# By-head norm, gate and turn of the second layer's attention output, with its gate kept on chip

## The reference, cut to what matters

```python
    a = p[:, 0] - lam * p[:, 1]                 # two softmaxes per head
    o = einsum('bhqk,bkhd->bqhd', a, v)
    o = rmsnorm(o, subln) * (1.0 - lambda_init) # per token and head, over 128 columns
    y = o.reshape(B, S, DIFF_WIDTH) * silu(gate)
    return y @ w_out
# and around it
    h = h + rmsnorm(y, norm_post[i])
```

## Time and profile before

| | us |
|---|---|
| runs of before | 2479.74, 2485.02, 2482.21 |
| median | 2482.21 |
| profiled execution, whole | 2479.8 |
| its span on the core | 2478.0 |
| PE busy | 2193.9 (89%) |
| DVE, ACT, POOL busy | 953.9, 873.6, 865.2 |

### The profile page before, as it was taken

How to read it: one execution, slowest core, us unless ns; L and a number is a source line. 1 busy time by engine, 2 the same in 40 slices (tenths; PEclk the granted TensorE clock), 3 DMA queues, 4 the chain that set the end, 5 groups by cost and what they waited for, 6 DMA issues and landing times. The chain is left out here.

```text
span 2478.0 us, 26013 instructions
## 1 busy us (share of the span) xinstructions
PE 2193.9 (89%) x10048; PEld 1736.3 (70%) x10048; DVE 953.9 (38%) x1603; ACT 873.6 (35%) x1740; POOL 865.2 (35%) x454
## 2 busy tenths in 40 slices
PE   4998999999957997857999999887987998999998
PEld 3877788888846775646677777675765456887876
DVE  1333334633453356553253411247552642210121
ACT  2544445655353554323232122231322222321231
POOL 3422233333314322244344433342224313444442
PEclk9999999999978999978999999898998998999999
DMA  4312122222332211222352233232223432332321
GB/s 154 100 53 69 52 84 71 86 86 81 129 110 75 90 52 58 70 85 85 102 149 89 86 86 94 73 102 69 81 79 124 131 113 66 96 103 85 102 90 64
DMA packets 130634, 221.32 MB, mean 89 GB/s; under 512 B 8744, under 2 KB 58456, under 8 KB 130304
## 3 DMA queue, kind: packets, MB, share of 16 engines
q1 hardware_dynamic: 110720, 168.63, 22.5%
q0 software_dynamic: 9104, 32.66, 4.0%
q10 hardware_dynamic: 10688, 18.35, 2.1%
HBM read 199.40 MB, written 19.62 MB: 88 GB/s over the span
## 5 line engine op out<-in xcount | busy, mean ns | idle before, releaser
L2238 POOL TENSOR_TENSOR lo_ring<-raw_ring,hi_ring 128x1024 fp32r<-128x1024 f32 (+1 forms) x304 | 732.0, 2430 | 1188.3 <-ACT hi_ring L1891 1188.2
L855 PE MATMUL bank<-xh,hi_ring 128*128 128x512 f32 x1472 | 601.7, 409 | 5.4 <-DVE xl L1337 3.3
L855 PE MATMUL bank<-xh,lo_ring 128*128 128x512 f32 x1472 | 582.4, 396 | 0.0
L855 PE MATMUL bank<-xl,hi_ring 128*128 128x512 f32 x1472 | 581.6, 395 | 0.0
L1891 ACT CAST hi_ring<-raw_ring 128x1024 fp32r<-128x1024 f32 (+1 forms) x304 | 303.4, 1046 | 512.9 <-PE bank L855 491.2
L855 PEld LDWEIGHTS bank<-xh,hi_ring 128*128 128x128 f32 x1472 | 282.5, 192 | 77.2 <-issue 18.5
L855 PEld LDWEIGHTS bank<-xh,lo_ring 128*128 128x128 f32 x1472 | 281.0, 191 | 61.5
L855 PEld LDWEIGHTS bank<-xl,hi_ring 128*128 128x128 f32 x1472 | 282.5, 192 | 57.8 <-issue 2.6
L855 PE MATMUL bank<-hi_ring,xh 128*128 128x512 f32 (+1 forms) x608 | 249.8, 411 | 11.4 <-POOL lo_ring L2238 6.4
L855 PE MATMUL bank<-hi_ring,xl 128*128 128x512 f32 (+1 forms) x608 | 242.2, 398 | 0.0
L855 PE MATMUL bank<-lo_ring,xh 128*128 128x512 f32 (+1 forms) x608 | 242.2, 398 | 0.0
(11 more groups left out here) (246 smaller groups left out, 2477.7 us busy)
## 6 DMA issues: line engine op xcount, KB each, us to landing
raw_ring<-in_ffn_w_in SPq DMA_DIRECT2D x176, 256.0 KB, 3.1
raw_ring<-in_dil_w_in SPq DMA_DIRECT2D x80, 512.0 KB, 3.7
raw_ring<-in_ffn_w_out SPq DMA_DIRECT2D x44, 512.0 KB, 3.8
raw_ring<-in_diff_w_in SPq DMA_DIRECT2D x32, 512.0 KB, 3.7
raw_ring<-in_w_in SPq DMA_DIRECT2D x32, 512.0 KB, 3.7
arena<-scratch_heads POOLq DMA_DIRECT2D x4, 1584.0 KB, 13.9
scratch_gates<-arena ACTq DMA_DIRECT2D x24, 256.0 KB, 2.1
arena<-scratch_gates POOLq DMA_DIRECT2D x24, 256.0 KB, 3.8
```

The costliest lines, as they stand in the source:

```text
L855: ins = T.matmul(bank[pb][:, 0:S if p.form == "feature" else p.cols], lhsT, rhs, start=(k == 0 and m == 0), stop=(k == p.K - 1 and m == le ...
L2238: G.tensor_tensor(lo, raw_ring[:, p % RAW, 0:q.kq * q.n], hi.bitcast(F32), ALU.subtract).then_inc(lowered, 1)
```

## The change

The list of jobs is different in four places, and four pieces of work are made anew.

- In the attention, the scores of tile n are put before the combine of tile n-1, the values of tile n-2 get the next step for themselves, and the turn of tile n-1 comes a step later, at the head of the step that holds the scores of tile n+1. This holds for both halves of the layer.
- Once a head's output is written, ACT squares it in four pieces of 128 columns with a sum each (o_square). DVE and POOL make the factor at the next head (o_mean).
- The gate goes to mix_gate, which lies in the first half's query and key tiles, and stays there. The store, the fetch and scratch_silu are gone. A head's output is multiplied by factor and gate at once on DVE, four instructions of 128 columns (o_weigh): for heads 0 to 3 behind macs 10, 12, 14 and 16 of the gate panels, for heads 4 to 7 after them.
- A head is turned into one bank by four transposes (o_turn), rounded with subln as the scale on ACT, and lowered on DVE with subln as the scale (o_lower). subln is now one value for each partition. Heads 0 to 3 are turned at once after the attention. Then come the four macs of the first step of the first y panel, which need chunks 0 to 3 only. Then follow, for each of the heads 4 to 7, o_weigh, o_turn and o_lower, and the second step waits for all of them (the field late).
- Both barriers go, the one after the attention and the one ahead of the output projection. The row norm_post now lies where o_sq was, and is loaded after the last squares.

```diff
-def finish_layer(plan, w, row_name, next_name):
-    plan.job("over", False)
-    plan.job("row", row_name)
-    for c in range(2):
+def finish_layer(plan, w, row_name, next_name, first=0):
+    if first == 0:
+        plan.job("over", False)
+        plan.job("row", row_name)
+    for c in range(first, 2):
...
         for n in range(N + 2):
+            if n < N:
+                plan.job("f_score", u, *jobs[n], banks=(4, 5))
             if 1 <= n <= N:
                 plan.job("f_combine", u, *jobs[n - 1])
-            if n < N:
-                plan.job("f_score", u, *jobs[n], banks=(4, 5))
+            yield
+            if n >= 2:
+                hh, i = jobs[n - 2]
+                plan.job("f_values", u, hh, i, banks=(7,) if i == 0 else ())
+                if i == NT - 1:
+                    plan.job("o_square", 4 * u + hh)
+                if i == 0 and hh:
+                    plan.job("o_mean", 4 * u + hh - 1)
             yield
             if 1 <= n <= N:
                 plan.job("f_turn", u, *jobs[n - 1], banks=(6,))
-            if n >= 2:
-                hh, i = jobs[n - 2]
-                plan.job("f_values", u, hh, i, banks=(7,) if i == 0 else ())
-            yield
+        plan.job("o_mean", 4 * u + 3)
...
-    interleave(gate_panels(plan, w, 3 * D, 1), side, 2.2)
-    plan.job("over", True)
-    plan.job("o_gate")
-    for n in range(NT):
-        plan.job("o_scale", n)
-    for n in range(NT + 1):
-        if n < NT:
-            plan.tile_parts("o_tile", n)
-        if n:
-            plan.job("lower", n - 1)
+    owed = 0.0
+    for step, _ in enumerate(gate_panels(plan, w, 3 * D, 1)):
+        owed += 2.2
+        while owed >= 1.0:
+            owed -= 1.0
+            next(side, None)
+        if step >= 9 and step % 2:
+            plan.job("o_weigh", (step - 9) // 2)
+    run_all(side)
+    plan.job("row", "post1")
+
+    def turn_head(h):
+        return ((f"drained{4 + h % 4}", plan.job("o_turn", h, banks=(4 + h % 4,))[0]),)
+
+    ready = [turn_head(h) for h in range(4)]
+    for h in range(4):
+        plan.job("o_lower", h)
+    plan.parts = (sum(ready, ()),) * NT
+    late = [(), (), (), ()]
+    main = plan.panel("y", "diff_w_out", 0, 512, "tile", at=(0,), late=late)
+    for _ in range(4):
+        next(main)
+    ready = []
+    for h in range(4, 8):
+        plan.job("o_weigh", h)
+        ready.append(turn_head(h))
+        plan.job("o_lower", h)
+    late[:] = [sum(ready, ())] * NT
+    run_all(main)
+    plan.parts = ((), (), (), ())
...
+                elif kind == "o_turn":
+                    h = a[0]
+                    T.wait_ge(o_weighed, h + 1)
+                    empty(4 + h % 4, job.use[0])
+                    for n in range(NT):
+                        ins = T.transpose(tile(bank[4 + h % 4], n), tile(O[:, n, :], h), ident)
+                    ins.then_inc(filled[4 + h % 4], 1)
...
+            def o_weigh(h):
+                V.wait_ge(o_rstd_made, h + 1)
+                V.wait_ge(drained[3], gate_panel[1, h // 4].use[3])
+                for n in range(NT):
+                    o_ = tile(O[:, n, :], h)
+                    ins = V.scalar_tensor_tensor(o_, o_, o_rms[:, 4 * h + n:4 * h + n + 1], tile(tile_gate(n, h // 4), h % 4), ALU.mult, ALU.mult)
+                ins.then_inc(o_weighed, 1)
+
+            def o_lower(job, h):
+                b = 4 + h % 4
+                V.wait_ge(o_rounded, h + 1)
+                V.scalar_tensor_tensor(xl[:, h, :], bank[b][:, :], subln, xh[:, h, :].bitcast(F32), ALU.mult, ALU.subtract).then_inc(drained[b], 1)
...
+                elif kind == "o_square":
+                    h = a[0]
+                    A.wait_ge(drained[7], use_of["f_values", 4 * NT * (h // 4) + NT * (h % 4)][0])
+                    if h:
+                        A.wait_ge(o_squared, h)
+                    for n in range(NT):
+                        ins = A.activation(tile(o_sq, n), tile(O[:, n, :], h), ACT.Square, accum_out=o_rms[:, 4 * h + n:4 * h + n + 1])
+                    ins.then_inc(o_squared, 1)
```

More of the change, by code:

```diff
@@ L83 @@
 Job = namedtuple("Job", "kind at n use")
-Panel = namedtuple("Panel", "kind at n w cols K form src use needs base")
+Panel = namedtuple("Panel", "kind at n w cols K form src use needs base late")
 Step = namedtuple("Step", "panel pieces k0 last end ahead")
@@ L119, in piece, with panel @@
         return len(self.pieces) - 1
-    def panel(self, kind, w, c0, cols, form, at=(), K=KC, src="x", k_first=0, halves=1, after=(), base=0):
+    def panel(self, kind, w, c0, cols, form, at=(), K=KC, src="x", k_first=0, halves=1, after=(), base=0, late=((),) * 4):
         parted = src in ("x", "hidden")
@@ L131, in panel @@
             needs = self.parts
-        self.panels.append(Panel(kind, at, n, w, cols, K, form, src, use, needs, base))
+        self.panels.append(Panel(kind, at, n, w, cols, K, form, src, use, needs, base, late))
         for first in range(0, K, 2 * KP):
@@ L554, in make_plan @@
     differential_layer(plan)
-    finish_layer(plan, "diff_w_out", "post1", "mix")
+    finish_layer(plan, "diff_w_out", "post1", "mix", first=1)
     ready = feed_forward(plan, "ffn1_w_in", "ffn1_w_out", before_hybrid(plan))
@@ L829, in mac @@
                     for name_value in p.needs[b]:
+                        T.wait_ge(*ready_value(name_value))
+                else:
+                    for name_value in p.late[b]:
                         T.wait_ge(*ready_value(name_value))
@@ L1260, in consume @@
                 m = 4 * p.n + o
-                if p.kind == "gate" and p.at[0] == 0:
+                if p.kind == "gate":
                     g = tile_gate(o, p.at[1])
@@ L1798, in vector_program @@
                     f_values(job, *a)
[L1799 to L1804, removed]
-                elif kind == "o_tile":
-                    o_tile(job, a[0])
+                elif kind == "o_mean":
+                    o_mean(a[0])
+                elif kind == "o_weigh":
+                    o_weigh(a[0])
+                elif kind == "o_lower":
+                    o_lower(job, a[0])
                 elif kind == "lot" and a[0] == 1:
@@ L1895, in consume @@
                 m = 4 * p.n + o
-                if p.kind == "gate" and p.at[0] == 0:
+                if p.kind == "gate":
                     A.wait_ge(filled[o], p.use[o])
                     A.activation(tile_gate(o, p.at[1]), psum, ACT.Tanh, scale=0.5).then_inc(gate_tanhed, 1)
-                elif p.kind == "gate":
-                    b, k = o % 2, 4 * p.at[1] + o
-                    A.wait_ge(filled[o], p.use[o])
-                    if k < 2:
-                        A.wait_ge(roped, 64)
-                    else:
-                        A.wait_ge(silu_stored[b], 16 * (k // 2))
-                    A.activation(rope_a[:, b, :], psum, ACT.Tanh, scale=0.5).then_inc(gate_tanhed, 1)
                 elif p.kind == "v":
@@ L2113, in scalar_program @@
                     ins.then_inc(third_weighed, 1)
-                elif kind in ("norm_tile", "mix", "o_tile"):
+                elif kind in ("norm_tile", "mix"):
                     round_tile(job, a[0])
@@ L2133, in scalar_program @@
                     copy_out(6, job.use[0], f_pt[:, job.n % 2, 0:nk], bank[6][:, 0:nk])
-                elif kind == "o_scale":
-                    A.activation(o_sq[:, a[0], :], O[:, a[0], :], ACT.Square).then_inc(o_squared, 1)
+                elif kind == "o_square":
[6 more added lines that the diff above has]
+                    ins.then_inc(o_squared, 1)
+                elif kind == "o_turn":
+                    h = a[0]
+                    A.wait_ge(filled[4 + h % 4], job.use[0])
+                    A.activation(xh[:, h, :], bank[4 + h % 4][:, :], ACT.Copy, scale=subln).then_inc(o_rounded, 1)
                 elif kind == "lot" and a[0] == 1:
@@ L2278, in gpsimd_program @@
                         splits(s)
-                    p = panels[steps[s].panel]
-                    if steps[s].last and p.kind == "gate" and p.at[0] == 1:
-                        layer, c = p.at
-                        G.wait_ge(drained[o], p.use[o])
-                        G.dma_start(scratch_silu[layer, o * P:(o + 1) * P, c * 512:(c + 1) * 512],
-                                    rope_a[:, o % 2, :]).then_inc(silu_stored[o % 2], 16)
                 elif kind == "over":
@@ L2305, in gpsimd_program @@
                 elif kind == "lambda":
-                    G.dma_start(rowv, I["rows"][0, ROWS["subln"][0]:ROWS["lk2"][1]].partition_broadcast(P)).then_inc(row_landed, 16)
-                elif kind == "o_gate":
-                    for b in range(2):
-                        G.wait_ge(silu_stored[b], 16 * 4)
-                    G.dma_start(o_gate, scratch_silu[1].rearrange("(n p) c -> p n c", p=P)).then_inc(o_gate_landed, 16)
-                elif kind == "o_scale":
-                    n = a[0]
-                    rstd(small[:, 16 + 8 * n:24 + 8 * n], o_meaned, n + 1, o_rstd_made)
```

(8 more changed lines are left out.)

48 lines of the change are left out of this document (20 added, 28 removed).

## The result

The changed kernel took 2470.62 us, the median of four runs (2469.68 to 2470.86). The kernel before took 2480.97, the median of its four runs. The ratio is 0.9948, with a 95% interval of 0.9932 to 0.9965, so the change gains 9 to 17 us of 2481. I had forecast 2461 (2450 to 2475). The time lies in the range, but the gain is 10 us where I had 21. The profiled execution took 2470.61, with a span of 2468.7 against 2478.0.

A forecast was written before the change was run, and what follows sets the result against it. PE and its pauses bound the kernel. Gains of 12.6 after the attention, 9 beside the gate panels and 0 beside the projections, 21.6 off 2479.8, with 2.4 added for the median, gave 2461 us (2450 to 2475).

The forecast's parts named there:

- the waits only move: Rival, attention beside the gate panels: PE's waits shift from f_turn to f_values, behind ACT, gaining 0; 2470 us, chance 0.20.
- part 2: Attention beside the gate panels: the later turn cuts PE's waits from 20.2 to about 13 us; gain 9, bounds 0 to 20.
- Part 1: After the attention, last values to end of output projection: 63.8 us against 76.4, gain 12.6, bounds 7.5 to 13.6.
- first step with its slow start: Output projection's first 48 matmuls: 10.9 us at full clock, plus 0.8 for half a low-clock restart.
- chain: Between the projection's first and second steps: heads 4 to 7 go one after another, three links of 3.3 us; 12.3 us.
- rest of y with its slow start: Output projection's second step and second panel: 144 matmuls, 32.7 us, plus 1.6 for the low-clock restart.
- The note that the early step hides nothing: After the attention: the early first step hides only head 4's weighing; with all turns ahead the sum would be 62.8 us.
- the rival of a longer chain: Rival, after the attention: links of 5 us take 5 us from the gain; 2466 us, chance 0.10.
- The 2 us for the clock: Beside the gate panels: low clock after waits costs 3 us of slower work before the change, 1 after.
- The eight stores bring nothing: Beside the gate panels: the gate's eight stores ended no wait of PE, so removing them brings nothing.
- Part 3: Attention beside the projections: waits for the combine mostly go, waits for the copy come; gain 0, bounds -5 to +5.
- POOL holds DVE: Rival, gate panels' stretch: POOL's subtractions hold up weighings and combines on DVE, about 7 us more; 2468 us, chance 0.07.

The follow-up runs named there:

- chain_first: The changed kernel with heads 4 to 7 weighed, turned and lowered ahead of the output projection's first four macs; 2468.21 us, ratio 0.994.
- old_order: The changed kernel with the attention's order of before in both halves, the rest of the change kept; 2472.01 us, ratio 0.9957.
- old_first_half: The changed kernel with the attention's order of before only in the half beside the projections; 2468.86 us, ratio 0.9931.
- turns_between: The changed kernel with weighings of heads 4 to 7 ahead of the first output step, their turns between its macs; 2457.06 us, ratio 0.9894.
- before_again: The kernel before, unchanged, run once more for a second trace; 2475.24 us, measured once.
- order_alone: The kernel before with only the new order of the attention in both halves; 2479.91 us, ratio 0.9976.
- after_again: The changed kernel, unchanged, run again for a second trace; 2471.28 us, ratio 0.9949.
- values_later: The changed kernel with the attention's values one tile later, tile n-3 where tile n-2 stood; 2468.12 us, ratio 0.9937.
- turns_between_again: The same kernel as turns_between, unchanged, run once more beside both_best; 2455.96 us, ratio 0.9873.
- both_best: The changed kernel with the edits of turns_between and old_first_half together; 2452.02 us, ratio 0.9867.

## Why the prediction was right or wrong

**What bounds the kernel.** Right: PE and its pauses; what was found lies in a pause or in the clock.

**The number.** The time lies in the range, but only half of the gain came. It stands almost on the 2470 of the rival "the waits only move", and that is chance: part 2 did not give 0. The two parts of the stage fell short by some 3 us each, and 6 us were lost outside it.

**Part 1, 12.6 forecast, 9.5 measured.** The mechanism was right to the link, the size was off in all four terms:

| term | forecast | measured |
|---|---|---|
| last values to first matmul of y | 5.5 | 5.7 |
| first step with its slow start | 0.8 + 10.9 | 12.6 |
| chain | 12.3 | 13.1 |
| rest of y with its slow start | 1.6 + 32.7 | 35.5 |
| sum | 63.8 | 66.9 |

The chain had three links, 3.2, 3.3 and 3.7 us, where I had 3.3; the last two turns took 1.12 at the half clock. The clock was the larger miss. I halved the first restart because its pause is short (3.87 us); eight matmuls at about 0.43 us and a few between cost it 1.7 all the same. The restart behind the chain cost 2.8, twelve matmuls at 0.43, where the earlier trace rows show eight. The note that the early step hides nothing is confirmed (chain_first: 64.5, where I had 62.8). What I failed to do was to ask of the chain, which I had named as the main point, whether it had to be: the rival of a longer chain weighed links of 5 us, and none of my cases took the chain for mere order.

**Part 2, 9 forecast, 7.8 measured.** The waits of the stretch are 11.4 us (6.5 and 4.9) where I had some 13 (5 and 8), a good size. The 2 us for the clock did not come: 0.95 before, 0.94 after, and PE was busy 0.8 us longer. "The eight stores bring nothing" is confirmed by old_order.

**Part 3, 0 forecast, a loss of 2.1 measured.** Inside the bounds. The copy behind ACT's work cost 6.4 us in four waits, where I had 5.4; the waits for the combine that I let go kept 3.8 of their some 6. With the old order there the whole attention is equally long, by fewer waits and a slower PE (old_first_half), so parts 2 and 3 are better read as one: 9 forecast, 5.7 measured. Of the difference 2 is the clock and 1.3 are waits: 7.2 less were forecast (20.2 to 13), 5.9 less measured.

**POOL holds DVE.** The longest combine took 2.63 us before, at the end of PE's wait of 6.43, and 1.93 after. One of 512 columns, 0.75 alone, took 1.80 after and ended a wait of PE of 2.13. In the tail it shows plainly: the first two of head 4's weighing instructions took 2.72 beside a subtraction of POOL's, where all four take 1.13 without POOL.

```profile
1064.84 2.72 DVE L1512 SCALAR_TENSOR_TENSOR arena<-arena,small 128x128 f32<-128x128 f32 x2
1064.91 2.50 POOL L2277 TENSOR_TENSOR lo_ring<-raw_ring,hi_ring 128x1024 fp32r<-128x1024 f32 x1 [1.49 <-ACT hi_ring L1926]
```

By the Trainium skill, "SBUF — State Buffer", section "Who interferes with whom", such a pair holds each other off; this row agrees for DVE, whose two end just after POOL's one. The four are done at 1070.2 and that head's turn starts at 1077.8, so it cost nothing here. The further 7 us that the rival gave did not appear beside the gates: that stretch has 11.4 us of waits where I had 13. In turns_between the same hold-off costs the two waits of 0.51 and 0.40.

**Outside the stage, 0 forecast, a loss of 6 measured.** The sum ended at the stage and assumed everything else to stay. Matched by their place in PE's order, the macs of each trace can be set against those of before. The stage is from the first rope mac beside the attention to the last matmul of y; us against the first trace of before:

| trace | lost ahead of the stage | gained in it | lost behind it |
|---|---|---|---|
| before_again | 1.5 | 5.1 | -1.0 |
| order_alone | 3.0 | 3.1 | -0.8 |
| after | 4.0 | 15.3 | 2.0 |
| after_again | 2.6 | 13.8 | 5.0 |
| old_order | 2.7 | 11.8 | 1.3 |
| old_first_half | 0.1 | 15.3 | 7.9 |
| values_later | -0.3 | 15.5 | 1.1 |
| chain_first | 0.1 | 17.6 | 7.1 |
| turns_between | 2.3 | 28.0 | 0.3 |
| turns_between_again | 0.6 | 27.9 | 3.4 |
| both_best | -0.3 | 27.7 | 0.0 |

The 4.0 ahead belong to the execution: 3.8 of them are there at 346 us, where the repeat has 0.2. What is lost behind is 0 to 8 us with the new tail, in steps of both signs, and 2.0 and 5.0 in two traces of one kernel. One step is the change's own. At a pause of PE between 1701 and 1737 us on the clock of before, 1.9 to 2.1 us are lost in all nine traces with the new tail, and none in before_again and order_alone. Within 0.3 they are won back by 1809. The pause is 14.4 us where it was 13.5. Two products of 448 columns on DVE, which take 1.15 without POOL, are held there; before, two of 384 were held, which take 0.55 each. First before, then after:

```profile
1706.89 1.84 DVE L1714 TENSOR_TENSOR arena<-arena,small 128x384 f32<-128x384 f32 x1
1708.65 2.69 DVE L1715 TENSOR_TENSOR arena<-arena,small 128x384 f32<-128x384 f32 x1
```
```profile
1694.75 5.45 DVE L1756 TENSOR_TENSOR arena<-arena 128x448 f32<-128x448 f32 x2
1694.60 5.11 POOL L2277 TENSOR_TENSOR lo_ring<-raw_ring,hi_ring 128x1024 fp32r<-128x1024 f32 x2 [6.70 <-ACT hi_ring L1926]
```

That is 3.4 us of holding before and 4.3 after, and the 0.9 between them is the pause's growth. The granted clock then stays at 0.50 for 3.4 us longer, which is the rest of the loss. POOL's pair starts 0.3 us earlier against PE's macs than before, and why it does stays open.

## What to carry to other kernels

When work is moved in front of a chain of small steps over several engines, write down each engine's queue first: here a weighing stood behind a lowering that it did not need, and four heads went one after another for 12.6 us that another order of the same jobs took away. Put the independent instructions of all items first, and the dependent ones one item behind, between pieces of long work. And price every pause of the matmul engine with its slow restart (1.7 and 2.8 us here), twice if the pause is cut in two.

## What the runs showed of the hardware

The same pause of some 2.3 us, in unchanged code, left the granted clock at 1.00 in eight of twelve traces and was followed by a fall to 0.50 in four, for nearly 7 us in one and for 3.4 us in three. Steps of 1.5 to 3 us of this kind, in places that differ from run to run, make up most of the difference between two traces of one kernel: executions of the kernel before ran from 2475.2 to 2494.2 us, and its attention took 204.2 us in one and 199.6 in another, with waits of 30.3 and 32.0. A DVE instruction held by a subtraction of POOL's is often off PE's path, but at three places it lengthened a wait of PE: at a combine of 1.80 us (0.75 alone), at the weighings of turns_between, and in the pause between 1701 and 1737 us. A change that moves 3 us can't be seen in medians of a few runs, but it can in the waits of the stretch that it touches. Less waiting is not always less time: in old_first_half and both_best some 2 us fewer waits went with 2.5 us more of PE's work at a lower clock.
